# Delta-rule block inverses: how the next X comes about in a two-layer hybrid diffusion backbone

## The reference, cut to what matters

```python
decay = jnp.where(incl, jnp.exp(jnp.where(incl, diff, 0.0)), 0.0)
kb = k * beta[..., None]
L = jnp.where(strict, jnp.einsum('bnhcd,bnhsd->bnhcs', kb, k) * decay, 0.0)
A = L + jnp.eye(C)
rhs = jnp.concatenate([v * beta[..., None], kb * jnp.exp(g)[..., None]], -1)
sol = lax.linalg.triangular_solve(A, rhs, left_side=True, lower=True, unit_diagonal=True)
```

## Time and profile before

| | us |
|---|---|
| median of 3 runs | 3415.96 |
| lowest and highest | 3412.11 and 3416.05 |
| span of the profiled execution | 3414.4 |
| TensorE busy | 3078.0 (90% of the span) |
| VectorE, ScalarE, GpSimd busy | 1462.5, 904.1, 1005.7 |

### The profile page before, as it was taken

How to read it: one execution, slowest core, us unless ns; L and a number is a source line. 1 busy time by engine, 2 the same in 40 slices (tenths; PEclk the granted TensorE clock), 3 DMA queues, 4 the chain that set the end, 5 groups by cost and what they waited for, 6 DMA issues and landing times.

```text
span 3414.4 us, 42364 instructions
## 1 busy us (share of the span) xinstructions
PE 3078.0 (90%) x17814; PEld 2614.0 (77%) x17814; DVE 1462.5 (43%) x2162; ACT 904.1 (26%) x1415; POOL 1005.7 (29%) x509
## 2 busy tenths in 40 slices
PE   2999999799978884789999998999999797889997
PEld 1888888688878883578888886888888566668886
DVE  7445555641535554536656656111111446431113
ACT  3211112222332223622112123211112226532222
POOL 3333333132211211213333332222222121234442
PEclk8999999898989996899999999999999999999998
DMA  5334343123200002223333332222121110123231
GB/s 203 96 108 138 120 144 125 64 99 110 79 21 1 1 1 80 66 68 118 126 140 124 133 129 73 63 66 61 59 66 59 54 56 1 34 78 97 89 97 63
DMA packets 118522, 282.39 MB, mean 83 GB/s; under 512 B 39614, under 2 KB 50622, under 8 KB 117950
## 3 DMA queue, kind: packets, MB, share of 16 engines
q1 hardware_dynamic: 116030, 273.39, 24.3%
q10 hardware_dynamic: 2304, 6.29, 0.5%
HBM read 268.07 MB, written 15.08 MB: 83 GB/s over the span
## 4 chain that ended last, share of the span: by engine, by line
PE 79%; DVE 8%; issue 5%; ACT 3%; POOL 2%; DMA 1%; SPq 1%; DVEq 0%; POOLq 0%; ACTq 0%
PE psum L1335 69%; PE psum L1438 2%; PE psum L1430 2%; PE psum L1515 1%; DVE ul L557 1%; PE psum L1522 1%; DVE prob_o L1279 1%; DVE sq L1104 1%; DVE rstd L1087 1%; PE psum L1367 1%; ACT prob_o L981 1%; POOL wl L722 1%; DMA raw<-in_w 0%; DVE probT_o L1288 0%; SPq L585 0%
## 5 line engine op out<-in xcount | busy, mean ns | idle before, releaser
L722 POOL TENSOR_TENSOR wl<-raw,wh 128x1024 fp32r<-128x1024 f32 (+1 forms) x329 | 847.6, 2577 | 1779.4 <-ACT wh L803 1779.4
L1335 PE MATMUL psum<-uh,wh 128*128 128x512 f32 (+1 forms) x3232 | 917.9, 353 | 111.9 <-DVE ul L557 103.6
L1335 PE MATMUL psum<-ul,wh 128*128 128x512 f32 (+1 forms) x3232 | 906.6, 350 | 0.0
L1335 PE MATMUL psum<-uh,wl 128*128 128x512 f32 (+1 forms) x3232 | 905.7, 350 | 0.0
L1335 PEld LDWEIGHTS psum<-uh,wh 128*128 128x128 f32 x3232 | 516.7, 190 | 217.2 <-issue 95.9
L1335 PEld LDWEIGHTS psum<-ul,wh 128*128 128x128 f32 x3232 | 517.0, 190 | 87.6 <-issue 1.7
L1335 PEld LDWEIGHTS psum<-uh,wl 128*128 128x128 f32 x3232 | 516.5, 189 | 86.8
L1051 DVE SCALAR_TENSOR_TENSOR ada_product<-ada_w,cb 128x1024 f32<-128x1024 f32 x256 | 486.5, 1900 | 8.5 <-DVE ada_product L1051 0.5
L803 ACT ACTIVATE wh<-raw 128x1024 fp32r<-128x1024 f32 (+1 forms) x329 | 337.9, 1028 | 441.0 <-PE psum L1335 387.8
L1119 DVE TENSOR_TENSOR af<-sg,psum 128x768 f32<-128x768 f32 (+1 forms) x88 | 78.1, 887 | 818.4 <-PE psum L1335 818.4
L1335 PE MATMUL psum<-al,wh 128*128 128x512 f32 x1232 | 342.3, 347 | 0.0
(11 more groups left out here) (192 smaller groups left out, 2413.1 us busy)
## 6 DMA issues: line engine op xcount, KB each, us to landing
raw<-in_w SPq DMA_DIRECT2D x264, 512.0 KB, 3.6
ada_w<-in_ada_w SPq DMA_DIRECT2D x128, 512.0 KB, 3.6
raw<-in_w SPq DMA_DIRECT2D x64, 448.0 KB, 3.3
ada_start<-in_ada_w SPq DMA_DIRECT2D x16, 512.0 KB, 16.4
spill<-cacc ACTq DMA_DIRECT2D x16, 384.0 KB, 2.3
ada_w<-bias_final SPq DMA_DIRECT2D x16, 256.0 KB, 3.0
h<-in_xT SPq DMA_DIRECT2D x1, 3072.0 KB, 14.6
bias_hbm<-toeplitz SPq DMA_DIRECT2D x192, 16.0 KB, 2.8
```

Of the source, the lines that this page charges most:

```text
L722: nc.gpsimd.tensor_tensor(wl[n % SPLIT_SLOTS][:, 0:k * w], raw[n % RAW_SLOTS][:, 0:k * w], wh[n % SPLIT_SLOTS][:, 0:k * w].bitcast(f32), A ...
L1335: ins = nc.tensor.matmul(pair[:, lo:hi], wt[n % SPLIT_SLOTS][:, k * P:(k + 1) * P], xt[:, k, lo:hi], start=first, stop=last)
```

## The change

The new X is no longer a transpose of the new Y. It is the product of the old Y (transposed by the matmul itself) and N, which is the same matrix. The X product therefore waits for N and not for the copy of the new Y. As it reads the old Y, ScalarE's copy of the new Y, which overwrites it, now waits for the X product (in level 6, which has no X, for its own product as before). Y of levels 2 to 6 gets a wait of its own for the copy of the Y before it.

```diff
@@ -927,7 +927,8 @@
                 elif x[0] == "dnY":
-                    act.wait_ge(product_done, i + 1)
+                    last_reader = ("dnX",) + x[1:] if x[3] < LEVELS - 1 else x
+                    act.wait_ge(product_done, number[last_reader] + 1)
                     nc.scalar.activation(dY[work(x)][:, :, :], pair4(banks_of(x), 0), ACT.Copy).then_inc(y_ready, 1)
@@ -1434,14 +1435,16 @@
                     pe.wait_ge(n_ready, no["dnN"][("dnN",) + x[1:]] + 1)
                     if k == 1:
                         pe.wait_ge(y1_ready, n + 1)
+                    else:
+                        pe.wait_ge(y_ready, no["dnY"][("dnY", x[1], d, k - 1)] + 1)
                     for hd in range(4):
                         ins = nc.tensor.matmul(pair4(pair, 0)[:, hd, :], dN[b][:, hd, :], dY[b][:, hd, :], start=True, stop=True)
                     ins.then_inc(product_done, 1)
                 elif x[0] == "dnX":
                     b = work(x)
-                    pe.wait_ge(y_ready, no["dnY"][("dnY",) + x[1:]] + 1)
+                    pe.wait_ge(n_ready, no["dnN"][("dnN",) + x[1:]] + 1)
                     for hd in range(4):
-                        ins = nc.tensor.transpose(pair4(pair, 0)[:, hd, :], dY[b][:, hd, :], ident[:, :])
+                        ins = nc.tensor.matmul(pair4(pair, 0)[:, hd, :], dY[b][:, hd, :], dN[b][:, hd, :], start=True, stop=True)
                     ins.then_inc(product_done, 1)
```

## The result

The changed kernel takes 3422.89 us (median of 10 runs, 3418.35 to 3425.57); the kernel before, now also in 10 runs, 3415.12 us (3408.83 to 3417.16). The ratio is 1.0022, 95% interval 1.0013 to 1.0030: slower by 7.8 us, with 4 to 10 us in the interval.

What follows compares the result with a forecast made beforehand. TensorE leads but isn't full; the chain N, Y, X, N sets levels without scan work. Levels +10.0 less clock falls 3.2 gives +6.8 us, from 3416.0 to 3422.8; 8-in-10 range 3417 to 3429.

Steps and rivals of the forecast that it cites:

- The price of the product: New X group on TensorE: 8 records instead of 4, 0.90 us instead of 0.45; 60 groups add 27 us of issue.
- Level by level: Sum over the 30 pairs of X groups: +10.0 us, with 17 of the added 27 us falling into idle time.
- The 14 levels: Levels with nothing between their products (2 to 5 of step 0, 4 and 5 of steps 1 to 5): +0.38 each, +5.3 us.
- Levels 1: Six levels, X to the next N from 1.48 to 1.93 us: +0.45 each, +2.7 us in all.
- Levels 2: Five levels: +0.41 each in steps 2 to 5, where `dnO` stands behind X, +0.39 in step 1; together +2.0 us.
- Levels 3: Five levels: no cost, since VectorE is still at `dnO` results when the product's results arrive; cover 0.76 us.
- The added waits: ScalarE's copy of Y waiting for X costs nothing: slack 2.2 us before the next Y needs the copy.
- The clock: Two of four falls to 1.2 GHz, at level 4 of steps 2 and 5, go: -3.2 us, bounds 0 and -6.4.
- Rival 1: The price is paid and the clock falls stay, or others come in their place: +10, 3426 us; chance 0.26.
- Rival 3: New X group no dearer than the transposes: -2.7 us, with two clock falls gone -5.9, 3410 us; chance 0.07.
- Rival 2: TensorE's queue order costs less than added, or more than two clock falls go: +2 to +5, 3419.5 us; chance 0.15.

## Why the prediction was right, point by point

The forecast was +6.8 us and 3422.8 us, the result is +7.8 and 3422.89. The mechanism is the one forecast, but that the absolute time fits to 0.1 us is luck: the kernel before is 0.8 us lower in 10 runs than in the 3 that I had, and two terms of the sum were too large, with opposite signs.

**The price of the product** was right in kind: 8 records a group, 0.90 us in a stream, X directly behind the second Y. The two experiments on records, twice the transposes and half the product, confirm it from both sides, at +11.0 (by the ratio +8.2) and -6.3 us. By the ratio of 4 that the Trainium skill's page "TensorE: Matmul & The Clock Gate" (section "Terms") gives for FP32 transposes, a product would have cost four transpose groups; here it costs two, and transposes issued twice cost the same.

**Level by level** the sum of +10.0 was too high by some 2 us.

- The 14 levels: +0.34 (5.75 against 5.41), not +0.38. Start of Y behind its mask takes 0.10, where I had carried over 0.15 from before. 0.6 us in all.
- Levels 1: in steps 2 and 5, for instance, Y to the next N went from 4.29 (1078.77 to 1083.06) to 4.74, and from 4.30 to 4.76, as forecast; in step 3 only from 4.45 to 4.74, since the second direction's Y was late there before (ScalarE takes the two Y results 1.12 us apart, at 1135.40 and 1136.52, instead of 0.90). In step 0 it is +0.26.
- Levels 2: +0.38 in step 4 (7.73 to 8.11 from N to N), forecast 0.41; in step 1 +0.30.
- Levels 3: nothing, as forecast; 8.98 before, 8.94 after in step 4, and free also by the run with the product in level 3 alone.

Steps 3 and 4, in which neither kernel has a fall, are 1.25 and 1.38 us longer, where I had 1.6. From these and step 0 (+1.6, of which about 0.1 is its first N at 0.50) the price is about 1.6 + 5 x 1.3 = 8.1 us; this takes the same 1.3 for the steps with a fall.

**The added waits** cost nothing, as forecast: the run with two buffers for Y is no faster.

**The clock.** Both falls at level 4 went, as said: steps 2 and 5 are 0.1 and 0.2 us shorter than before in spite of the price of about 1.3, so a fall cost some 1.5 us, where I had 1.6. What I hadn't in the sum: the fall near 1023 us, in the masks ahead of step 1, moved to 1029 us, into level 1 (the window of 1029 above is at 0.50, which is 1.2 GHz). Step 1 is 3.4 us longer for it, of which 0.8 come back before it (`dnV` to the first N 13.14 instead of 13.91). In the stretch the balance is 8.1 - 3.0 for two falls + 1.3 or so for the moved one, 6.4 of the 6.5 us that the two profiles show. What the prediction left out is that a fall costs more in one place than in another: near 1023 it had cost next to nothing. The kernel with the product in level 3 alone, with no fall there, takes 49.6 us from `dnV` of step 0 to `dnV` of step 1, the kernel before 49.8. Without the fall N of direction 1 waits 1.32 us for GpSimd's mask instead (before 0.55), which the prediction had as ready before level 1. The forecast of +6.8 thus holds, but with a price too high by 1.9, and a clock that gave back less than I had.

Over many executions the two gaps at level 4 are worth less than the 3.0 us of these two profiles. Of 8 idle times of 2.33 to 2.36 us before a level's N in three profiles (before, half product, transposes with the scan before X) 5 were followed by a fall, none of 8 of 1.45 to 1.49 us (the change, doubled transposes, product in level 3, two buffers for Y) and none of 8 of 1.61 to 1.64 us. As an estimate from these counts the two gaps give back 2 x 5/8 x 1.5 = 1.9 us on average, not 3.2: 8.1 - 1.9 = 6.2 us beside the measured 7.8 with 4 to 10 in its interval. What lies between the two isn't settled; the clock elsewhere in the program is a part of every run.

The Trainium skill's page "TensorE: Matmul & The Clock Gate", Part 4 ("PE-mode transpose"), says that transposes don't count as busy time for the clock as matmuls do. The trace of before agreed with it as well as with idle time. The run with doubled transposes speaks against it (3.39 us of transposes and idle time, no fall in either of two steps), and so does the half product, whose gap of 2.34 us behind products had a fall. With so few gaps it is not disproved.

**Rivals.** Rival 1, the price paid and the falls still there or others in their place, can't be told from my forecast by the times: +10 lies at the edge of the interval. The trace decides, in one execution each: no fall at level 4, a price of 8.1 and not 10, but one fall that moved to a dearer place, as this rival allowed. Rival 3 named the right lever: at 4 records a group the change is 6.3 us faster than before, where I had worked out 5.9 (its profile has other falls than that of the change, so a part of the 6.3 may be the clock). Its condition isn't met by the real product. Rival 2 (order of TensorE's queue) isn't borne out.

## What to carry to other kernels

Trading a transpose for a product shortens a chain only on paper, as long as the order stays, when the engine that runs both is nearly full: count its records per level first, here 4 more for each group, against the idle time that the removed link leaves (0.8 us a level against 0.9 of new work for two groups). Where a chain of TensorE and eviction steps has work of another kind to mix in, the place of that work in VectorE's order is worth more than the link: moving the scan products `dnU` and `dnO` between N and Y gained 15.7 us with an unchanged set of instructions, and moving them between Y and X lost 5.9. The clock has a small part in this: the profile of the new order has no fall at level 4 but one at the start of step 5, one fewer in all, about 1.5 of the 15.7 us. Test a saved link and its price apart, by doubling the cheap form and by halving the dear one.

## What the runs showed of the hardware that I had not expected

The clock falls behind some idle times and not behind others of the same length. Before N of a level, behind 2.33 to 2.36 us it fell 5 times in 8, behind 1.61 to 1.64 us never in 8 and behind 1.45 to 1.49 us never in 8. Among the short bursts ahead of a step even less was followed by one: behind the 1.32 us before the second N of step 1 it fell 3 times in 7 (the change, doubled transposes, product in the order N, scan, Y, X), and behind the 1.84 us that TensorE waits before the first N of steps 2 to 5 it fell 7 times in 52 (13 profiles, 4 steps each), never in those of before and of the change. I had read the 2.36 us of one profile as a sure fall. So single profiles of kernels that differ by a few us can be apart by some 1.5 us for each fall, in either direction: the changed kernel's profile is 2.6 us longer in span than that of before, its median 7.8 us.
